# Hybrid retention and HGRN2 layer: the HGRN2 recurrence with the logarithm of the keys inside its exponents, GpSimd's differences ordered by direction, and the decayed queries moved behind the levels

## What is computed

```
def hg_dir(p, z, lb):
    q = silu(to_heads(p[4]))
    f = lbh + (1.0 - lbh) * sigmoid(to_heads(z))
    return q, 1.0 - f, to_heads(p[7]), log(f)          # q, k, v, log_a
# S_t = diag(a_t) S_{t-1} + k_t v_t^T ;  o_t = S_t^T q_t, chunkwise:
b = cumsum(log_a)
scores = einsum('bhtsd,bhsd->bhts', q[t] * exp(b_t - b_s), k)     # s <= t
out    = scores @ v + (q * exp(b)) @ state
new_state = exp(b_end) * state + (k * exp(b_end - b))^T v
```

## Time and profile before

| | us |
|---|---|
| median of 3 runs | 2729.41 (2728.48 to 2729.89) |
| profiled execution, its own time | 2731.74 |
| its span | 2729.8 |
| PE busy | 2571.3 (94%) |
| DVE busy | 2054.5 (75%) |
| ACT busy | 1455.5 (53%) |
| POOL busy | 542.8 (20%) |
| DMA queues, share of 16 engines | 57.7% and 7.0% |

### The profile page before, as it was taken

One profiled execution on the slowest core, in us unless ns is written; L12 is line 12 of the kernel. 1 busy time (PEld: TensorE's weight loads), 2 busy tenths in 40 slices (PEclk: granted clock), 3 DMA queues, 4 the chain that ended last, 5 costly groups with the idle time before them and its releaser, 6 DMA issues.

```text
span 2729.8 us, 45966 instructions
## 1 busy us (share of the span) xinstructions
PE 2571.3 (94%) x16329; PEld 2201.9 (81%) x16330; DVE 2054.5 (75%) x2515; ACT 1455.5 (53%) x1648; POOL 542.8 (20%) x423
## 2 busy tenths in 40 slices
PE   7998987999897999999999999999999999999995
PEld 3896766777886788877887979899989897898885
DVE  5437788545677896999879788766686778968786
ACT  5446665213443664777647565644454456645554
POOL 0035565200023211122121111111111212112111
PEclk9999988999997999999999999999999999999998
DMA  7121111442244996999969788766586678968793
GB/s 290 39 88 37 30 42 57 160 165 93 89 88 133 346 380 212 382 358 356 318 234 364 266 300 278 272 224 208 191 304 209 236 262 313 354 206 293 266 318 134
DMA packets 274965, 607.07 MB, mean 222 GB/s; under 512 B 21837, under 2 KB 52981, under 8 KB 273761
## 3 DMA queue, kind: packets, MB, share of 16 engines
q1 hardware_dynamic: 254496, 562.41, 57.7%
q0 software_dynamic: 20384, 43.51, 7.0%
HBM read 582.87 MB, written 46.97 MB: 231 GB/s over the span
## 4 chain that ended last, share of the span: by engine, by line
PE 36%; issue 11%; DVE 9%; ACT 5%; DMA 4%; SPq 1%; DVEq 1%; POOL 1%; ACTq 0%; POOLq 0%
PE e_acc L2609 7%; PE e_acc L2612 7%; PE e_acc L2610 7%; PE e_acc L2582 4%; PE e_acc L2584 4%; PE e_acc L2583 4%; DVE e_slot_r L2765 3%; ACT whi L2693 3%; DMA list_now<-lists 3%; SPq L2341 1%; PE e_tb L2551 1%; DVE yo L2851 1%; DVE e_alo L2774 1%; DVE e_glu L2827 1%; DMA slot<-in_w 1%
## 5 line engine op out<-in xcount | busy, mean ns | idle before, releaser
L2693 ACT ACTIVATE whi<-e_slot 128x2048 fp32r<-128x2048 f32 x296 | 561.5, 1914 | 395.2 <-PE e_acc L2612 327.0
L2765 DVE TENSOR_TENSOR e_slot_r<-e_slot,whi 128x2048 fp32r<-128x2048 f32 x296 | 674.9, 2287 | 114.2 <-ACT whi L2693 114.2
L2609 PE MATMUL e_acc<-e_xhi,whi 128*128 128x256 f32 x1664 | 398.9, 282 | 4.5 <-ACT e_xhi L2697 4.5
L2693 ACT ACTIVATE whi<-slot 128x2048 fp32r<-128x2048 f32 x148 | 283.2, 1913 | 180.5 <-PE e_acc L2584 180.2
L2765 DVE TENSOR_TENSOR slot_r<-slot,whi 128x2048 fp32r<-128x2048 f32 x151 | 344.3, 2282 | 24.4 <-ACT whi L2693 21.8
L2582 PE MATMUL e_acc<-whi,e_ahi 128*128 128x512 f32 x800 | 320.3, 400 | 4.3 <-DVE e_glu L2827 4.3
L2609 PEld LDWEIGHTS e_acc<-e_xhi,whi 128*128 128x128 f32 x1664 | 313.2, 188 | 7.6 <-ACT e_xhi L2697 7.6
L2584 PE MATMUL e_acc<-whi,e_alo 128*128 128x512 f32 x800 | 313.3, 392 | 0.0
L2583 PE MATMUL e_acc<-e_slot_r,e_ahi 128*128 128x512 f32 x800 | 311.4, 389 | 0.0
L2509 POOL DMA_INDIRECT sum<-yo,e_idx_now x48 | 118.5, 2470 | 949.7 <-issue 505.9
L2582 PE MATMUL e_acc<-whi,e_xhi 128*128 128x512 f32 x768 | 304.4, 396 | 1.3 <-DVE e_slot_r L2765 1.1
(11 more groups left out here) (449 smaller groups left out, 4993.3 us busy)
## 6 DMA issues: line engine op xcount, KB each, us to landing
e_slot<-in_w SPq DMA_DIRECT2D x296, 1024.0 KB, 7.6
slot<-in_w SPq DMA_DIRECT2D x151, 1024.0 KB
rv<-in_w_ada SPq DMA_DIRECT2D x32, 512.0 KB, 5.4
slot<-in_w_in SPq DMA_DIRECT2D x9, 1024.0 KB, 9.7
wa<-in_w_ada SPq DMA_DIRECT2D x8, 1024.0 KB, 17.1
slot<-in_w_in SPq DMA_DIRECT2D x12, 512.0 KB, 4.4
xt<-in_x SPq DMA_DIRECT2D x8, 512.0 KB, 14.8
slot<-in_w_out SPq DMA_DIRECT2D x4, 1024.0 KB, 14.2
```

Of the source, the lines that this page charges most:

```text
L2609: pe.matmul(out[:, c, :], whi[i % RING][:, w], xhi[:, kk, :], start=first, stop=False, skip_group_check=True)
L2693: act.activation(whi[i % RING][:], raw[i % PIECES][:], ACT.Copy).then_inc(S["whi_made"], 1)
L2765: v.tensor_tensor(wlo[i % PIECES][:], raw[i % PIECES][:], whi[i % RING][:].bitcast(F32), ALU.subtract).then_inc(S["wlo_made"], 1)
```

## The change

1. The keys become logarithms. ScalarE takes sigmoid(-z) (`key_sigmoids`), from it log f as before with a scale of -(1 - lb) and a bias of 1 (`gate_logs`), and then, in place, log of ((1 - lb)·sigmoid(-z) + 1e-36) (`key_logs`). VectorE subtracts `cum` from it, or adds `ahead` (`keys`). All key exponents take this sum as input and give k·exp(...) at once: `key_decays` (one direction per call now), the key half of `first_level`, and GpSimd's key differences. `decayed_keys` and the two key products of `level` are gone.
2. The sum of the two directions' keys is made from the sigmoids before they are overwritten (`sum_keys`, two operations of 512 per half) in a buffer of its own, `key_sum`.
3. GpSimd's differences go by direction: for levels 1 to 6 the forward query difference, then forward keys, then by level backward query and key. It waits for the forward sums alone before it starts. `roots` of the head before come behind level 3.
4. The forward scan has five pieces of 256 in place of three.
5. The orders change: at a passage VectorE does `level 0`, `finish`, levels 1 and 2, `states(0)`, the early low halves, levels 3 to 6, `states(1)`, and only then `decayed_queries`; ScalarE does first level queries and the copy of the first turned keys before the squares, and `query_decays` last; TensorE does `gates_of_keys(h + 2, 0)` behind the second group of turned keys; high and low chunk 3h+6 come earlier.

```diff
+            def key_logs(h, half):
+                act.wait_ge(S["key_sums"], 2 * h + half + 1)
+                act.wait_ge(S["logf"], 4 * h + 4)
+                for d in range(2):
+                    x = key_pieces(h, d)[half][0]
+                    act.activation(x, x, ACT.Ln, scale=bound[:, h, d, 1:2], bias=offset[:, 1:2]).then_inc(S["key_logs"], 1)
...
             def keys(h, d):
-                v.wait_ge(S["logf"], 4 * h + 2 * d + 2)
-                for x, _ in key_pieces(h, d):
-                    v.tensor_scalar(x, x, bound[:, h, d, 2:3], bound[:, h, d, 1:2], ALU.mult, ALU.add).then_inc(S["keys_ready"], 1)
+                v.wait_ge(S["cumulated"], 6 * h + 3 * d + 3)
+                for half, (x, _) in enumerate(key_pieces(h, d)):
+                    v.wait_ge(S["key_logs"], 4 * h + 2 * half + d + 1)
+                    if d:
+                        k = v.tensor_tensor(tiles(x), tiles(x), ahead_pieces(h)[half][0][:, :, 0:P], ALU.add)
+                    else:
+                        k = v.tensor_tensor(x, x, cum_pieces(h)[half][0], ALU.subtract)
+                    k.then_inc(S["keys_ready"], 1)
...
+            def sum_keys(h, half):
...
+                v.tensor_scalar(to, k0, bound[:, h, 0, 1:2], None, ALU.mult).then_inc(S["summed"], 1)
+                v.wait_ge(S["summed"], 2 * h + half + 1)
+                v.scalar_tensor_tensor(to, k1, bound[:, h, 1, 1:2], to, ALU.mult, ALU.add).then_inc(S["key_sums"], 1)
...
             def level(h, half, l):
...
-                v.tensor_tensor(k4[:, :, 0], k4[:, :, 0], view(k0, hl)[:, :, 0], ALU.mult).then_inc(S["lev_mul"], 1)
-                v.tensor_tensor(k4[:, :, 1], k4[:, :, 1], view(k1, hl)[:, :, 1], ALU.mult).then_inc(S["lev_mul"], 1)
-                v.wait_ge(S["lev_exp"], at + 2 * l + 2)
+                v.wait_ge(S["lev_exp"], 2 * NL * (2 * h + half) + 2 * l + 1)
                 v.tensor_tensor(wq[:, l, :], wq[:, l, :], q[:, lo:lo + HN], ALU.mult).then_inc(S["lev_ready" if l == NL - 1 else "lev_mul"], 1)
```

GpSimd, in `levels`:

```diff
+                g.wait_ge(S["cumulated"], 6 * h + 3)
+                for l in range(1, NL):
+                    difference(l, "q", 0)
+                g.wait_ge(S["keys_ready"], 4 * h + 2)
+                for l in range(1, NL):
+                    difference(l, "k", 0)
+                g.wait_ge(S["cumulated"], 6 * h + 6)
+                for l in range(1, NL):
+                    difference(l, "q", 1)
+                    if l == 1:
+                        g.wait_ge(S["keys_ready"], 4 * h + 4)
+                    difference(l, "k", 1)
+                    if l == 3 and roots_of is not None:
+                        roots(roots_of, 1)
```

TensorE's loop over heads:

```diff
                     for n in range(6):
                         turn_keys(h + 1, n)
+                        if n == 1 and h + 2 < HEADS:
+                            gates_of_keys(h + 2, 0)
                     updates(h + 1)
                     if h + 2 < HEADS:
-                        gates_of_keys(h + 2, 0)
                         gates_of_keys(h + 2, 1)
```

ScalarE's loop over heads:

```diff
                 if more:
-                    logs(h + 1)
-                    key_decays(h + 1)
+                    key_sigmoids(h + 1)
+                    gate_logs(h + 1)
+                    key_logs(h + 1, 0)
+                    if h + 2 < HEADS:
+                        high_chunk(3 * h + 6)
+                    key_logs(h + 1, 1)
                     query_sig(h + 1, 0)
+                    key_decays(h + 1, 0)
+                    query_sig(h + 1, 1)
+                    first_level(h + 1, 0, "queries")
+                    turned_keys(h + 1, 0)
...
                 roots(h, 1)
                 if more:
...
+                    key_decays(h + 1, 1)
+                    turned_keys(h + 1, 1)
+                    first_level(h + 1, 0, "keys")
+                    turned_keys(h + 1, 2)
                     totals(h + 1)
-                    for n in range(6):
+                    for n in range(3, 6):
                         turned_keys(h + 1, n)
-                        levels(h + 1, 0, ((), (0,), (), (1,), (), (2,))[n])
+                        levels(h + 1, 0, (n - 2,))
                     if h + 2 == HEADS:
                         high_early(0)
                         high_early(1)
-                    levels(h + 1, 0, range(3, NL))
+                    levels(h + 1, 0, range(4, NL))
+                    query_decays(h + 1)
                     gate_sig(h + 1)
```

VectorE's loop over heads (`now` is h >= 0, `more` is h + 1 < HEADS):

```diff
+                    if more:
+                        sum_keys(h + 1, 0)
                     pick(h, HT)
...
                 if more:
                     cumulate(h + 1, 0)
+                    middles(h + 1, 0)
...
                 if now:
                     pick(h, HT + 1)
                     pick(h, HT + 2)
-                if more:
-                    cumulate(h + 1, 1)
-                if now:
+                    if more:
+                        sum_keys(h + 1, 1)
+                    if more and h + 2 < HEADS:
+                        low_chunk(3 * h + 6)
                     pick(h, HT + 3)
                 if more:
                     keys(h + 1, 0)
-                    decayed_keys(h + 1, 0)
+                    cumulate(h + 1, 1)
+                    middles(h + 1, 1)
                     keys(h + 1, 1)
-                    decayed_keys(h + 1, 1)
...
+                        level(h + 1, 0, 0)
+                        finish(h, 1)
+                        level(h + 1, 0, 1)
+                        level(h + 1, 0, 2)
+                        states(h + 1, 0)
+                        if h + 2 == HEADS:
                             low_early(0)
                             low_early(1)
+                        for l in range(3, NL):
+                            level(h + 1, 0, l)
+                        states(h + 1, 1)
+                        decayed_queries(h + 1, 0)
+                        decayed_queries(h + 1, 1)
```

More of the change, by code:

```diff
@@ L438, in hgrn2 @@
         MADE = [2, 1]
-        gout = [at(f"h_gout{i}", PAIR, first_at + 8 * WSLOT + 4 * PAIR * i, F32) for i in range(2)]
-        assert first_at + 8 * WSLOT + 8 * PAIR <= first_end and early_at + 8 * WSLOT <= wk_at
+        gout = [at("h_gout0", PAIR, first_at + 8 * WSLOT, F32), at("h_gout1", PAIR, st_at, F32)]
+        assert first_at + 8 * WSLOT + 4 * PAIR <= first_end and early_at + 8 * WSLOT <= wk_at
+        assert wk_at + 8 * WSLOT + 16 * 512 <= first_at
         W, w_in = keep["h_W"], keep["h_w_in"]
@@ L726, in scores @@
                 if i == 0:
+                    pe.wait_ge(S["key_sums"], 2 * h + half + 1)
+                    pe.wait_ge(S["lev_exp"], 2 * NL * (2 * h + half + 1))
                     pe.wait_ge(S["lev_ready"], 2 * h + half + 1)
-                pe.matmul(out[:, 0:P], wk[:, NL, i * P:(i + 1) * P], q[:, j * P:(j + 1) * P], start=True, stop=True)
+                pe.matmul(out[:, 0:P], key_sum[:, j * P:(j + 1) * P], q[:, j * P:(j + 1) * P], start=True, stop=True)
                 for l, hl in enumerate(LEVELS[:2]):
@@ L904, in totals @@
             def totals(h):
+                act.wait_ge(S["states"], 2 * (LT + 1) * h)
                 for x, part in cum_pieces(h):
@@ L943, in early_rows, with first_level @@
                 act.activation(keep["rqk"][:, row_of(x), :], pj[x % 2][:], ACT.Copy).then_inc(S["rows_taken"], 1)
-            def first_level(h, half):
+            def first_level(h, half, part):
                 act.wait_ge(S["s_done"], LT * h + half * HT)
@@ L967, in levels @@
                     if l == 0:
-                        first_level(h, half)
+                        first_level(h, half, "queries")
+                        first_level(h, half, "keys")
                         continue
-                    act.wait_ge(S["lev_sub"], DIFF * h + half * DIFF // 2 + 4 * l)
-                    for x in (wk, wq):
+                    done = DIFF * h + half * DIFF // 2 + 2 * (NL - 1) + 2 * l
+                    for x, n in ((wq, done - 1), (wk, done)):
+                        act.wait_ge(S["lev_sub"], n)
                         act.activation(x[:, l, :], x[:, l, :], ACT.Exp).then_inc(S["lev_exp"], 1)
@@ L1002, in _ @@
             act.wait_ge(S["bounds"], 3)
-            logs(0)
+            key_sigmoids(0)
+            gate_logs(0)
             value(4)
+            for half in range(2):
+                key_logs(0, half)
             value(5)
-            key_decays(0)
+            key_decays(0, 0)
             value(6)
@@ L1072, in _, with levels @@
         def _(g):
-            def levels(h, half, which):
+            def levels(h, half, roots_of=None):
                 g.wait_ge(S["s_done"], LT * h + half * HT)
@@ L1077, in levels, with difference @@
                     values_out(g)
-                for l in which:
+                def difference(l, of, d):
                     hl = LEVELS[l]
@@ L1082, in levels @@
                     fwd, bwd = by_tile(tiles(latent_cum(h, half))), by_tile(latent_ahead(h, half))
```

(9 more changed lines are left out.)

157 lines of the change are left out of this document (79 added, 78 removed).

## The result

| | before | after |
|---|---|---|
| median, us | 2729.57 (8 runs) | 2739.63 (8 runs) |
| profiled execution, its span, us | 2729.8 | 2736.1 |
| DVE busy, us | 2054.5 | 1988.5 |
| ACT busy, us | 1455.5 | 1468.6 |
| POOL busy, us | 542.8 | 521.4 |

The change makes the kernel slower: 1.0035 times the time of before (95% interval 1.0024 to 1.0046). The forecast was 2725.0 with a range up to 2738.

The account below looks back on a forecast made before the run. TensorE was taken to bound the recurrence, with waits only where heads pass. Two passages of 0.4 us and 3.6 at the last make 4.4 us less than the median 2729.41: 2725.0 us, range 2714 to 2738.

Parts of the forecast that it names:

- Work: Whole recurrence: VectorE loses some 80 us net, almost none of it on the path by itself.
- The wait for po: Passage head 1 to 2: TensorE waits for VectorE's finish to free bank po, about 9 us against 4.4, ending 4.6 later.
- Gate product in the gap, turns, updates: Passage 1 to 2: head h+2's gate product fills ScalarE's copy gap; scores may start at 370.9, 1.2 us gained.
- No wait of scores for level products: Passage 1 to 2: VectorE's level products end at 368.8, before TensorE's scores may start at 370.9.
- The decayed queries before the first pick: Passage 1 to 2: VectorE's two take 2.4 to 3.2 us ahead of the pick; passage gains 0 to 0.8, taken 0.4.
- my walk: Engine-by-engine timing of passage 1 to 2 in before's trace times, putting the first output's pick at 375.6 to 376.4.
- the half clock: Gate product behind the po wait, passage 1 to 2: partly at half granted clock, 1.6 us more taken.
- The last passage: Passage 2 to 3: early rows start at 449.1 against 452.69, 3.6 us gained.
- Rival A: GpSimd's key differences double VectorE's backward scans, 3.3 us later, three passages of 4.1: 2737.3 us; chance 0.17.
- the signs I had named for being wrong: Profile after: po wait not longer, scans or additions at twice their length, or a TensorE gap in head 0's front.

Follow-up runs that it names:

- experiment 1: Changed kernel with the decayed queries back ahead of the levels, right behind finish on VectorE, their exponents earlier on ScalarE: 2729.75 us, ratio 0.9996 to the kernel before.
- experiment 5: Changed kernel with GpSimd's two output-gate products waiting until the decayed queries are made: 2731.69 us, ratio 1.0001 to the kernel before.
- Experiment 3: Changed kernel with the third tile's scores of heads 1 to 3 made four times, filling TensorE's wait before the first output: 2736.81 us, ratio 1.0025.
- experiments 2 and 6: Changed kernel, GpSimd's forward key differences waiting for the backward scans: 2739.38 us; the same plus its gate products waiting for the decayed queries: 2731.55 us.
- experiment 4: Kernel before with only the decayed queries and their exponents of heads 1 to 3 moved behind levels and second states: 2742.27 us, ratio 1.0047.

## Why the prediction was wrong

The forecast was 2725.0; measured 2739.63. Step by step:

- **Work.** VectorE's busy time fell by 66 us, not 80. Three passages of doubled scans (3.0 us each) and the decayed queries (4.52 in place of 3.19 us) account for some 12 of the 14. That almost none of the work removed is on the path held: with the queries early (experiment 1) the time is that of before, within its interval.
- **The wait for po.** Forecast as the wait that takes the place of the old one, about 9 us; measured 9.78. It ends 2.2 us later than walked, since the scans took 3.0 us more and the roots 1.3 us in place of 2, and it begins 1.5 us later, behind the sixth tile's output.
- **Gate product in the gap, turns, updates.** Scores were to start 1.2 us earlier against the last gate product of head 1; they started 0.1 earlier (6.0 us of shift to that product, 5.9 to the scores). The 1.5 us from the sixth pick, which I had not followed past the scans, are in it. No wait of scores for level products: right.
- **The decayed queries before the first pick: the step that failed.** The place was seen, "VectorE stands before it with the second states ... and now both decayed queries", and the first output was named as what waits. The size was 2.4 to 3.2 us, and "I take 0.4" of gain. Measured: 4.52 us, and the output 2.9 us later than before in the frame of that last gate product. Against my walk the output came 3.3 us later (in that frame at 379.4; walked 375.6 to 376.4). 1.6 us of it stood ahead of the two queries already (they began at 373.8 in place of 372.2, behind the po wait that ended later), the rest is their length. My 3.2 us for the contested case is what the two took in the kernel before (3.19) beside level differences; here the neighbour is GpSimd's gate products, which had stood elsewhere. Without that neighbour they take 2.36 us (experiment 5), and most of the loss is gone.
- **What the wait costs behind it: left out.** I used the half clock once, for the gate product behind the po wait (1.6 us taken; turn and product ran from 361.3 to 366.2 at 0.68, 4.9 us for 3.6 warm, so 1.3). I did not ask the same of the new wait at the first output: 2.6 us more. So the step put at 0.4 us of gain per passage was a loss of 5.5 us at passage 1 to 2 (2.9 and 2.6) and of 5.8 at 0 to 1 (3.9 and 1.9), each counted from the last gate product ahead. Experiment 3 shows the clock's part, experiment 5 the contention's, experiment 1 that moving the queries takes all of it away.
- **The last passage.** Forecast 3.6 gained, measured 2.7. Right in kind and nearly in size.
- **Rival A.** "The scans are slowed by GpSimd" was true as a mechanism, at the size given (3.0 us for 3.3), and its time, 2737.3, lies near the measured one; twice the length of a scan was also one of the signs I had named for being wrong. That the time is near is luck. It is not the cause of the loss: in experiment 1 the scans are as slow and the loss is gone, and in experiments 2 and 6, where the scans are fast, nothing comes back for it. It does have a part in the 1.6 us above, through the later end of the po wait. The Trainium skill, "GPSIMD Engine Reference", section "Key points", says that GpSimd contends with instructions of VectorE that have two SBUF inputs; the trace agrees for scans (4.33 against 2.00 us for six). My reason against it, that a scan leaves room since it takes twice a product's time per element, was wrong.

The clock also shows how near such a case lies to none: in experiment 5 a wait of 1.49 us was followed by the full clock, in experiment 4 one of 1.55 by 0.63. In the changed kernel itself the sixth tile's output waits 1.58 us in head 0 and 1.57 in head 1; behind the first it takes 1.19 us until the gate product, behind the second 1.83, and from 340.19 to 343.10 the granted clock is 0.56. What decides between them no run here was made to show.

## What to carry to other kernels

Work put at the end of an engine's queue because "it is needed last" must be checked against the next small operation that another engine waits for: 4.5 us of products stood ahead of a pick of 1 us, with 10 us of idle time earlier in the same queue. A new wait on TensorE is priced with the slow stretch behind it: here 2.6 us lost behind a wait of 3.6. And taking a contention away is worth nothing while something on the path stands behind the work that was put off: the same 3 us of scans per passage gave 0 in two experiments, where GpSimd's roots came behind the delayed differences, and 4 us in a third, where they came first.

## What the hardware showed that was not expected

- Scans of VectorE double beside GpSimd's differences: six of 128 elements 4.33 us against 2.00, and GpSimd's six differences of 256 are 4.80 beside scans and 5.75 beside additions, so neither place leaves them at the 4.15 us that six take elsewhere (386.54 in experiment 3, where VectorE is idle or does picks for most of the time).
- Products of 1024 elements on both engines slow each other: VectorE's two 4.52 against 2.36 us, GpSimd's first 3.07 against 2.35 in experiment 5.
- After TensorE had been idle for 3.63 us, outputs and scores ran at a granted clock of 0.50 for all of 6.2 us; with 4.78 us of work put into 5.93 us ahead of them they ran at 1.00.
